# Expert loop with units of 32 and 64 rows by turns in place of units of 64

## What is computed

```python
logits = tok @ w_router + b_router            # 512 x 32
top_logit, top_idx = lax.top_k(logits, 4); top_w = softmax(top_logit)
# for each expert e, on the rows of the tokens that picked it:
gu = xe @ w_gate_up[e] + b_gate_up[e]         # rows x 2048
gate = minimum(gu[:, :1024], 7.0); up = clip(gu[:, 1024:], -7.0, 7.0)
act = (up + 1.0) * gate * sigmoid(1.702 * gate)
y = act @ w_down[e] + b_down[e]               # rows x 1024
# the token's output is the sum of its four y, weighted by top_w
```

## Time and profile before

| what | us |
|---|---|
| median of 3 runs (3197.66 to 3199.18) | 3198.24 |
| the profiled execution | 3199.99 |
| its span, first to last instruction | 3198.2 |
| expert loop, first to last gate-and-up product | 1063.3 to 2214.3 |
| TensorE busy (share of the span) | 3104.2 (97%) |
| DVE, ACT, POOL busy | 1321.6, 841.0, 341.5 |

### The profile page before, as it was taken

The page is one execution under the profiler, slowest core; times in us unless marked ns, Lnnn a source line. Parts: engine busy times, 40 slices in busy tenths (PEclk is TensorE's granted clock), DMA queues, the critical chain, the costliest instruction groups (busy, mean ns, idle before and its releaser), DMA issues.

```text
span 3198.2 us, 40985 instructions
## 1 busy us (share of the span) xinstructions
PE 3104.2 (97%) x14106; PEld 1837.5 (57%) x14107; DVE 1321.6 (41%) x2126; ACT 841.0 (26%) x1605; POOL 341.5 (11%) x313
## 2 busy tenths in 40 slices
PE   7999999999999999999999999999999999999999
PEld 5555556564888433333333333333787888888887
DVE  2465554754345312121212121221566587444552
ACT  3264453620212111111111111111325445211100
POOL 0112021421001000000000000000301444000000
PEclk9999999999999999999999999999999999999999
DMA  5324233246124699999999997796320121222121
GB/s 215 120 83 134 84 125 125 105 189 216 73 79 154 247 370 386 381 386 395 388 385 382 382 393 281 286 386 243 144 101 32 66 83 34 102 79 93 53 79 56
DMA packets 190022, 632.85 MB, mean 198 GB/s; under 512 B 18752, under 2 KB 56000, under 8 KB 179168
## 3 DMA queue, kind: packets, MB, share of 16 engines
q1 hardware_dynamic: 161216, 552.79, 45.1%
q0 software_dynamic: 10944, 39.85, 3.5%
q10 hardware_dynamic: 17760, 38.78, 3.4%
HBM read 594.78 MB, written 36.57 MB: 197 GB/s over the span
## 4 chain that ended last, share of the span: by engine, by line
PE 85%; DMA 5%; DVE 5%; ACT 2%; issue 2%; SPq 1%; ACTq 0%; DVEq 0%
PE ps L322 25%; PE ps L2348 17%; PE ps L2322 11%; PE ps L2034 9%; PE ps L271 6%; DMA slot<-in_w_exp 5%; PE ps L2086 2%; PE ps L2577 2%; PE ps L2095 2%; PE ps L2549 1%; PE ps L1964 1%; PE ps L2532 1%; PE ps L2317 1%; SPq L1366 1%; PE ps L2313 1%
## 5 line engine op out<-in xcount | busy, mean ns | idle before, releaser
L2348 PE MATMUL ps<-slot,xT_blk 128*64 128x512 f32 x3200 | 735.1, 600 | 28.4 <-DMA slot<-in_w_exp 26.4
L2348 PEld LDWEIGHTS ps<-slot,xT_blk 128*64 128x64 f32 x3200 | 218.7, 137 | 465.7 <-issue 377.5
L2322 PE MATMUL ps<-slot,aT 128*64 128x512 f32 x1632 | 363.9, 599 | 0.9 <-ACT aT L1725 0.9
L2034 PE MATMUL ps<-hT,slot 128*128 128x512 f32 (+1 forms) x896 | 307.6, 502 | 0.8 <-DVE sum_row L2679 0.8
L2322 PEld LDWEIGHTS ps<-slot,aT 128*64 128x64 f32 x1632 | 117.5, 138 | 238.9 <-issue 238.8
L3113 DVE TENSOR_TENSOR gate<-ps,b_row 128x512 f32<-128x512 f32 x50 | 34.6, 691 | 517.8 <-PE ps L2348 517.6
L2034 PEld LDWEIGHTS ps<-hT,slot 128*128 128x128 f32 x896 | 168.3, 190 | 128.9 <-issue 120.1
L2707 DVE SCALAR_TENSOR_TENSOR conv<-ps,g_conv,conv 128x510 f32<-128x510 f32 (+1 forms) x224 | 133.3, 631 | 179.7 <-ACT conv L1507 176.3
L3109 DVE MEMSET b_there<- 128x1 f32 x50 | 3.0, 59 | 388.6 <-DMA b_few<-in_b_gu 381.2
L1700 ACT ACTIVATE y_row<-ps 128x512 f32<-128x512 f32 x51 | 30.4, 597 | 384.3 <-PE ps L2322 384.3
L322 PE MATMUL ps<-in_t,in_s 128*128 128x264 f32 x528 | 124.8, 386 | 0.5 <-issue 0.5
(11 more groups left out here) (512 smaller groups left out, 4673.9 us busy)
## 6 DMA issues: line engine op xcount, KB each, us to landing
slot<-in_w_exp SPq DMA_DIRECT2D x768, 512.0 KB, 8.6
in_w<-in_w_ffn SPq DMA_DIRECT2D x22, 1024.0 KB, 4.8
expert_rows<-zero SPq DMA_DIRECT2D x4, 4608.0 KB, 22.1
slot<-in_w_xbc SPq DMA_DIRECT2D x8, 2048.0 KB, 7.6
sum_here<-sum_rows ACTq DMA_DIRECT2D x32, 512.0 KB, 3.6
w_modT<-in_w_modT POOLq DMA_DIRECT2D x32, 512.0 KB, 3.9
rnn_w<-in_w_rnn SPq DMA_DIRECT2D x16, 1024.0 KB, 4.8
expert_rows<-y_row ACTq DMA_DIRECT2D x102, 128.0 KB, 5.5
```

The lines of the kernel that those rows point to most:

```text
L2034: last = pe.matmul(ps[:, 2 * (m % 2) + part, 0:n], w[:, (k * 4 + m % 4) * P:(k * 4 + m % 4 + 1) * P], hT[:, k, c0:c0 + n], start=(k == 0), ...
L2322: last = pe.matmul(ps[h * UNIT:(h + 1) * UNIT, 6, :], aT[:, t, d * UNIT:(d + 1) * UNIT], slot[4 + d][:, t * D + h * 512:t * D + (h + 1) * ...
L2348: last = pe.matmul(ps[h * UNIT:(h + 1) * UNIT, 2 * s + t, :], xT_blk[:, k, s * UNIT:(s + 1) * UNIT], slot[i // 4][:, at:at + 512], start=( ...
```

## The change

- Units have 32 rows for s = 0 and 64 for s = 1. 96 rows are gathered per turn of the loop, and units are taken in the order of the experts' indices. An expert takes units, from wherever the sequence stands, until they hold its rows.
- A 32-row unit uses four column groups of 32: a gate-and-up piece is still two products of 512 columns, to groups 0 and 1 for an even piece and 2 and 3 for an odd one; a down piece is four products of 256 columns. The columns of gate and up in the pieces are rearranged for it. A unit accumulates gate and up in one bank (s = 0) or two (s = 1); `y_row`, `aT`, `b_row` and `b_few` exist once for each size.
- Activations are turned behind eight pieces and the down product comes behind ten; TensorE's wait for the second half of the rows moves to directly behind the turning. DVE's first instruction waits for `gu15`.
- A 32-row result is stored in four transfers of 32 x 256. The bias of an expert is eight rows for SP in place of four.
- The routing gets other steps: units counted for both starting sizes, the size at which each expert starts by a scan, no order to work out and no product "rows"; tables are wider (46 and 89 columns for 34 and 66), spots narrower (96 for 128).

With the counts above this makes the sequence (32 and 64 by turns) 1 unit for experts 0, 1, 4, 11, 21, 22, 23, 30, 31; 3 for 7, 9, 24; 4 for 20; 2 for all others: 60 units. Units of 64 rows are 50: 1 for 16 experts, 2 for 14, 3 for 20 and 24.

```diff
-UNIT = 64
-UNITS = SEQ * TOPK // UNIT + NE - 1
+UNIT_ROWS = [32, 64]
+UNIT_AT = [0, 32]
+PERIOD = 96
+TILES = [P // n for n in UNIT_ROWS]
+PART = D // TILES[0]
+PERIODS = -(-(SEQ * TOPK + NE * (UNIT_ROWS[1] - 1)) // PERIOD)
+UNITS = 2 * PERIODS
...
-    TURN_AT, DOWN_AT = 5, 6
+    TURN_AT, DOWN_AT = 8, 10
...
+    GATE_PS = [ps[:, 2:3, :], ps[:, 0:2, :]]
+    AT_BANK, Y_BANK_OF = [3, 5], [7, 6]
...
+    def store_unit(act, i, s):
+        rows, first = UNIT_ROWS[s], i * PERIOD + (UNIT_ROWS[1] if s == 0 else 0)
+        width = D // TILES[s]
+        for j in range(TILES[s]):
+            act.dma_start(expert_rows[bass.ds(first, rows), j * width:(j + 1) * width],
+                          y_row[s][j * rows:(j + 1) * rows].rearrange("p t c -> p (t c)")).then_inc(s_yrow[s], 16)
...
         def load_bias(e):
-            for h in range(2):
-                for p in range(h * UNIT, (h + 1) * UNIT, 32):
-                    sp.dma_start(b_few[p:p + 1].rearrange("p t f -> p (t f)"), io["b_gu"][bass.ds(e * 2 + h, 1), :]).then_inc(s_brow, 16)
+            for j in range(TILES[0]):
+                sp.dma_start(b_few[0][j * 32:j * 32 + 1].rearrange("p t f -> p (t f)"), io["b_gu"][bass.ds(e * TILES[0] + j, 1), :]).then_inc(s_brow, 16)
+                sp.dma_start(b_few[1][j * 32:j * 32 + 1].rearrange("p t f -> p (t f)"),
+                             io["b_gu_64"][bass.ds(e * TILES[1] + j // 2, 1), :]).then_inc(s_brow, 16)
...
-        def down(d, t):
-            for h in range(2):
-                last = pe.matmul(ps[h * UNIT:(h + 1) * UNIT, 6, :], aT[:, t, d * UNIT:(d + 1) * UNIT],
-                                 slot[4 + d][:, t * D + h * 512:t * D + (h + 1) * 512],
-                                 start=(d == 0 and t == 0), stop=(d == 1 and t == 3))
+        def down(k, s):
+            quarter, c = divmod(k, 2)
+            half, tile = divmod(quarter, TILES[s])
+            rows, width = UNIT_ROWS[s], D // TILES[s]
+            for j in range(TILES[s]):
+                at = k % 4 * D + j * width
+                last = pe.matmul(ps[j * rows:(j + 1) * rows, Y_BANK_OF[s], 0:width], aT[s][:, 2 * half + c, tile * rows:(tile + 1) * rows],
+                                 slot[4 + k // 4][:, at:at + width], start=(k == 0), stop=(k == DN_PIECES - 1))
             return last
...
                         for h in range(2):
                             at = i % 4 * PIECE + h * 512
-                            last = pe.matmul(ps[h * UNIT:(h + 1) * UNIT, 2 * s + t, :], xT_blk[:, k, s * UNIT:(s + 1) * UNIT],
+                            half, tile = divmod(2 * t + h, TILES[s])
+                            rows, first = UNIT_ROWS[s], UNIT_AT[s]
+                            last = pe.matmul(GATE_PS[s][tile * rows:(tile + 1) * rows, half, :], xT_blk[:, k, first:first + rows],
                                              slot[i // 4][:, at:at + 512], start=(k == 0), stop=(k == KD - 1))
...
                 gate_up(range(TURN_AT))
                 pe.wait_ge(moe_dve.sem, moe_dve.before("act", u))
                 moe_pe.done(turn_act(1 - s), "aT")
+                if s == 0:
+                    pe.wait_ge(moe_xT_act.sem, moe_xT_act.before("half1", i))
                 gate_up(range(TURN_AT, DOWN_AT))
...
-                gate_up(range(DOWN_AT, 8))
                 if s:
                     turn_x(0)
-                if s == 0:
-                    pe.wait_ge(moe_xT_act.sem, moe_xT_act.before("half1", i))
-                gate_up(range(8, GU_PIECES))
+                gate_up(range(DOWN_AT, GU_PIECES))
```

## The result

The kernel before took 3197.95 us (median of 4), the changed one 3171.73 us (3169.28 to 3173.28): ratio 0.9911, 95% interval 0.9898 to 0.9923, or 26 us less. Forecast were 12 us less (3186 us, range 3170 to 3222). The sign was right and the time lies just inside the lower end of the range, but the gain is more than twice the forecast. Run again, the changed kernel took 3174.65 us (ratio 0.9928), a little more than the 3169 to 3174 expected of it.

The account below looks back on a forecast made before the run. The loop was taken as bound by weights and TensorE in turn, with weights a 1082 us floor after the change. Span 3198.2 - 14.3 (loop) + 1.3 (before it) + 0.7 (behind it) = 3185.9, set at 3186 us; range 3170 to 3222.

Parts of the forecast that it names:

- Two limits in turn: Expert loop before: bound by weights from 1230 to 1900 us, by TensorE from 1925 to 1985 us.
- four column groups at full rate: 32-row products: four start per 0.43 us, so gate and up take 6.86 us and the down product 3.43 us.
- one block of weights behind each one-unit expert: Loop: after each of seven one-unit experts TensorE waits for the next block, 15 to 20 us each.
- the cost behind the loop: After the last products: last chain starts one product pair step later, +0.7 us; the last down pieces' arrival is hidden.
- the price of a block of weights: Loop after the change: fetching one expert's weights with gather, stores and bias takes 34.9 us; 31 blocks make a 1082 us floor.
- 0.45 us per expert: Loop before: remainder of the 69.5 us two-expert cycle over the priced 68.6 us, put down to small packets and gaps.
- the walk: Piece-by-piece reckoning of the loop, 1.355 us per piece, 2 us from free place to transfer: 1152.7 us before, 1138.4 after.
- TensorE's turn: Loop: TensorE's work on one 32-row and one 64-row unit, 34.3 us plus 0.4 for feeding the down product, 34.7 us.
- The slope: Loop: up to 0.5 us more per turn costs under 5 us in all; each further microsecond about 24.
- Rivals 1 and 2: 1: TensorE not fed in 32-row down product, 3211 us, chance 0.20; 2: losses half as large, 3198 us, chance 0.16.
- rival 3: Gate and up: four column groups below full rate, 3213 us, chance 0.04; only two at once, 3348 us, chance 0.02.
- Rival 4: Loop: weights come faster, blocks take 34.4 us, walk 1125 to 1128, kernel 3175 us; chance 0.10, within faster.

Follow-up runs that it names:

- the redone walk: The prediction's piece-by-piece reckoning with 1.333 us per piece and 3 us from free place to transfer: loop 1156.2 us before, 1123.8 after; measured 1153.9 and 1125.9.
- four more labellings: Changed kernel, experts relabelled: order rotated by 12, 3188.65 us; by 3, 3201.35; by 6, 3222.92; an order searched with the walk, 3140.27.
- rotated by 6: Experts relabelled in the order 6, 7, ... 31, 0, ... 5: kernel before 3207.43 us, changed kernel 3222.92 us.
- searched labels: Changed kernel with experts relabelled in an order searched with the walk for these tokens, 56 units in place of 60: 3140.27 us, ratio 0.9835.

## Why the prediction was right, and where it was wrong

**Right: the frame.** Two limits in turn; 60 units in 30 turns; four column groups at full rate; one block of weights behind each one-unit expert; waits for weights up to some 70 us (80 forecast), with clock drops; activations just covered (waits of its weight loads up to 1.1 us, next to none of products); the cost behind the loop +1.2, with the last chain 1.4 later (0.7 was forecast).

**Wrong: "I take 34.9 us", the price of a block of weights.** The step that failed is the reading that from 1230 to 1900 us, at 99%, the loop "is bound by the weights", and with it the 0.45 us per expert that the prediction put down as "left over (small packets, gaps)". A block is 33.3 us in the kernel before, where 34.75 was put, and 34.3 to 34.4 in the changed one, where 34.9 was put. The same section's rows had the counter-evidence in sight: a share of 1.03 and 410 GB/s over 3.4 us against 0.99 and 386. Two shorter stretches of the kernel before say the same, 1.03 and then 0.93 in one and the same cycle:

```profile
1155.00:1165.00 10.00, 8.84 (x40) 2.59 (x42) 1.02 (x2) 2.02 (x3) 0.67 (x2) 1.00 1.03 413
...
1185.00:1195.00 10.00, 10.00 (x50) 3.57 (x48) 0.00 (x0) 1.74 (x5) 0.00 (x0) 1.00 0.93 348
```

The cycle of 69.5 us was thus set by TensorE and the fetches handing over to each other. I fitted one number (the piece) to it and guessed the other (2 us from free place to transfer). From 1930 to 1985 us, where the engines are far from full (0.65 in the earlier trace rows), an issue took 6.4 us to land, which leaves 5.1 us beside a transfer of 1.28; no run isolates this term. Two pairs, 1.355 and 2 us or 1.333 and 3, give the loop of before within 2.5 us; after, they give 1133.2 and 1123.8. The agreement of the walk with the 1151 us of before confirmed neither. Nor does that of the redone walk with the changed kernel: its block of 33.4 to 33.7 us is 0.7 to 1 us too cheap there, so errors cancel in its 1123.8, and how far is not shown.

**Mis-sized: TensorE's turn,** 34.7 for 33.98. The 0.4 us for feeding the 32-row down product are not there (3.59 us with its change of width, where 3.97 were put), and turnings of 96 rows cost 0.1 us less each. The step out of the 64-row products costs 0.15 us (1504.99 - 1503.12 - 4 x 0.43), as the 0.14 taken. The Trainium skill's 62 ns per MATMUL in one mode ("TensorE: Matmul & The Clock Gate", section on the gap of 56 ns) would have made it an estimated 4.0 us; the trace has 56 ns per product (3.59 us for 64), so that price doesn't apply here. That a change of tiling mode drains TensorE (the Trainium skill, "TensorEngine Tiling (Array Packing)", Key Properties) agrees with the 0.15 us; the page gives no size.

**The slope** ("up to 0.5 us more per turn costs under 5 us in all") followed from the same wrong price: 0.44 us more cost 6.3, 0.9 us more cost 16.4. Rivals 1 and 2 rested on the turn and are refuted, rival 3 too: four column groups start per 0.43 us with a wait ahead of each two products. Rival 4 (weights faster) had the size of the block, 34.4 us, and with it a loop of 1125 to 1128 and 3175 us, against 1125.9 to 1129.1 and 3172 to 3175 measured; I gave it 0.10. The range's lower end came from it, and that is why the range held.

**Missed altogether:** how much hangs on the labels. The walk could have said so blind, and a single permuted list would have shown that the forecast's -14 us was one draw from a wide set. Redone walks over 150 random labellings give the changed kernel's loop 1157 +- 18 us and the old one 1154 +- 1 (an estimate from the walk; the table above has four more labellings, measured). The 1154 +- 1 can't hold where the planner's first expert is a heavy one: rotated by 6, the old kernel's loop took 1165.3 us.

**Open:** what the half-clock stretches cost (the forecast said 0, bound 12; no run separates it); why a block of the changed kernel costs some 1 us more than one of before; and the time from a free place to the transfer, 2 or 3 us in the walks, which no run shows.

The best of the kernels is the changed one with the searched labels, 3140.27 us; it fits this routing only. One that serves any routing would have to choose its sequence from the counts, as the planner of the kernel before did; that was not tried.

## What to carry to other kernels

A resource is full when its share reads what it reads in a stretch where nothing else can be the limit; find that reading in the same trace before a price is divided out of a "99%". Look at the time from issue to landing, too: if it grows, the queue is falling behind. A model with two unknown prices that meets one measured number has confirmed neither: look for a second stretch that moves them apart, and put both pairs into the range. Where a schedule depends on the data, run the model over permuted data too, before a gain is credited to the change.

## What the hardware showed that I had not expected

- The DMA share of a saturated stretch reads 1.02 to 1.03, at 390 to 413 GB/s according to the mix; 0.99 with 387 GB/s was short of it, since an eighth less work on TensorE raised it to 1.02 and 403.
- A row of issues at an even distance does not show that the transfers keep up. Over six blocks 33.98 us apart the time from issue to landing grew from 10.0 to 12.1 us.
- 64 products and 64 weight loads of 128x32 by 256 columns went through in 3.59 us, 28 ns an instruction, with a change of group width in it.
- Warming products can lie on the path themselves: the 30 records ahead of the first turn took 6.7 to 9.5 us by the clock, with the rows' turning right behind them.
